# Two in-order queues reordered around a split-precision feed-forward layer, and a third pair of operand slots between its down passes

## What is computed

```
def swiglu(h, w_gate, w_up, w_down):
    return (jax.nn.silu(h @ w_gate) * (h @ w_up)) @ w_down
h = rms_norm(x, ffn1_norm[i])
x = x + 0.5 * swiglu(h, ffn1_w_gate[i], ffn1_w_up[i], ffn1_w_down[i])
```

## Time and profile before

| | us |
|---|---|
| timed runs, median (lowest to highest) | 914.07 (912.55 to 914.72) |
| profiled execution, its own time | 912.49 |
| its span, first to last instruction | 910.7 |
| DVE, ACT, POOL busy in it | 541.8, 496.5, 475.3 |

### The profile page before, as it was taken

The page is one execution under the profiler, slowest core; times in us unless marked ns, Lnnn a source line. Parts: engine busy times, 40 slices in busy tenths (PEclk is TensorE's granted clock), DMA queues, the critical chain, the costliest instruction groups (busy, mean ns, idle before and its releaser), DMA issues.

```text
span 910.7 us, 15441 instructions
## 1 busy us (share of the span) xinstructions
PE 893.5 (98%) x5462; PEld 798.7 (88%) x5462; DVE 541.8 (59%) x819; ACT 496.5 (55%) x777; POOL 475.3 (52%) x228
## 2 busy tenths in 40 slices
PE   9989999999999999999999999999999999989998
PEld 7779999999988778887788879999999988878887
DVE  7586766676422733778958586667666522652552
ACT  5765666566433633668834756556655533433451
POOL 0446666666554364266665346666665564355430
PEclk9999999999999999999999999999999999999999
DMA  7523333333333244221324233333333253223311
GB/s 200 160 59 115 115 92 98 110 115 92 109 122 92 70 115 102 60 81 48 70 70 120 65 93 93 101 106 114 92 106 103 90 162 93 91 92 93 94 69 46
DMA packets 131049, 89.33 MB, mean 98 GB/s; under 512 B 11552, under 2 KB 116296, under 8 KB 131016
## 3 DMA queue, kind: packets, MB, share of 16 engines
q1 hardware_dynamic: 131000, 88.90, 32.9%
q10 hardware_dynamic: 16, 0.00, 0.0%
HBM read 86.80 MB, written 2.10 MB: 98 GB/s over the span
## 4 chain that ended last, share of the span: by engine, by line
PE 86%; DVE 7%; ACT 4%; issue 2%; DMA 0%; SPq 0%; DVEq 0%; ACTq 0%
PE bank L1586 28%; PE bank L1587 28%; PE bank L1588 28%; PE bank L1601 1%; DVE wx_lo L1117 1%; ACT act_f L579 1%; DVE x_t L1194 1%; ACT w_hi L530 1%; DVE tmp L1192 1%; PE bank L1857 1%; DVE w_lo L1083 1%; DVE act_f L1129 0%; ACT tmp L575 0%; DMA raw<-in_ffn_w_up 0%; DVE h_lo L1022 0%
## 5 line engine op out<-in xcount | busy, mean ns | idle before, releaser
L405 POOL TENSOR_TENSOR w_lo<-raw,w_hi 128x1024 fp32r<-128x1024 f32 x85 | 219.2, 2587 | 246.1 <-ACT w_hi L530 246.1
L1586 PE MATMUL bank<-h_hi,w_hi 128*128 128x256 f32 (+1 forms) x700 | 228.2, 326 | 3.9 <-DVE w_lo L1083 3.9
L1588 PE MATMUL bank<-h_hi,w_lo 128*128 128x256 f32 (+1 forms) x700 | 226.8, 324 | 0.0
L1587 PE MATMUL bank<-h_lo,w_hi 128*128 128x256 f32 (+1 forms) x700 | 226.8, 324 | 0.0
L1117 DVE TENSOR_TENSOR wx_lo<-act_f,wx_hi 128x1024 fp32r<-128x1024 f32 x44 | 65.7, 1497 | 145.7 <-ACT wx_hi L631 145.6
L1586 PEld LDWEIGHTS bank<-h_hi,w_hi 128*128 128x128 f32 x700 | 133.2, 190 | 16.0 <-DVE w_lo L1083 4.8
L1588 PEld LDWEIGHTS bank<-h_hi,w_lo 128*128 128x128 f32 x700 | 133.3, 190 | 10.7
L1586 PE MATMUL bank<-wx_hi,w_hi 128*128 128x512 f32 x352 | 137.9, 392 | 4.9 <-DVE wx_lo L1117 4.9
L1587 PEld LDWEIGHTS bank<-h_lo,w_hi 128*128 128x128 f32 x700 | 133.3, 190 | 10.0
L1587 PE MATMUL bank<-wx_lo,w_hi 128*128 128x512 f32 x352 | 137.7, 391 | 0.0
L1588 PE MATMUL bank<-wx_hi,w_lo 128*128 128x512 f32 x352 | 137.5, 391 | 0.0
(11 more groups left out here) (232 smaller groups left out, 1891.0 us busy)
## 6 DMA issues: line engine op xcount, KB each, us to landing
raw<-in_ffn_w_down SPq DMA_DIRECT2D x44, 512.0 KB, 3.7
raw<-in_ffn_w_gate SPq DMA_DIRECT2D x42, 512.0 KB, 3.8
raw<-in_ffn_w_up SPq DMA_DIRECT2D x42, 512.0 KB, 3.8
raw<-in_w_ple_gate SPq DMA_DIRECT2D x8, 512.0 KB, 3.7
...
```

Of the source, the lines that this page charges most:

```text
L405: pool.tensor_tensor(w_lo[:, slot, :], raw[:, slot, :], f32(w_hi[:, slot, :]), ALU.subtract).then_inc(w_ready, 1)
L1586: nc.tensor.matmul(dst, a_hi, b_hi, start=first, stop=False, skip_group_check=more)
L1587: nc.tensor.matmul(dst, a_hi, b_lo, start=False, stop=False, skip_group_check=more)
L1588: return nc.tensor.matmul(dst, a_lo, b_hi, start=False, stop=last, skip_group_check=more)
```

## The change

- Seam, ACT: the eight h_gained run as one block, so that the splits of chunks 6 and 7 come behind all eight; the copies for the weight sums (rstd, stage, u, g, sa) come ahead of the x_rounds and silu(2), and u_round ahead of g_round.
- Seam, DVE: x3 and x2 come ahead of plain_up(1), then sums(2, 0) and u_rest; x4, the x_rests and block 2 of the plain part follow. plain_up(2) stands ahead of x_rest(2).
- Meet: a third pair of buffers, wx_hi[:, 2] and wx_lo[:, 2], which the seven-block pairs use for g and which is free by then, takes chunk 11. act_split(11) needs no wait; act_split(12) waits for chunk 9 and act_split(13) for chunk 10, each one chunk earlier than before; from 14 on the slots alternate again, and act_split(ch) waits for chunk ch - 2. On DVE act_rest(13) stands ahead of the four updates and act_rest(14) behind the four h_rests. On ACT act_split(14) stands ahead of split(15), counted in down chunks, and split(16) follows it. The loops of the second pass are written out.

The slots, and the waits of act_split:

```
+        def act_slot(ch):
+
+            return ch % 2 if ch < DH else 2 if ch == DH else (ch + 1) % 2
...
+                if ch < 2:
+                    act.wait_ge(w_used, c0 + GU - 2)
+                elif DH < ch < DH + 3:
+                    act.wait_ge(w_used, c0 + GU + ch - 2)
+                elif ch != DH:
+                    act.wait_ge(w_used, g + c0 + GU - 1)
```

ACT and then DVE at the seam:

```
-                for d in range(HALF):
+                for d in range(KD):
                     h_gained(n, d)
                 split(c0 + SLOTS + 2)
-                for d in range(HALF, KD):
-                    h_gained(n, d)
                 split(c0 + SLOTS + 3)
                 silu(n, 1, tmp[:, 1, :])
-                x_round(n, 0)
-                x_round(n, 1)
-                silu(n, 2, tmp[:, 0, :])
-                x_round(n, 2)
...
                 stage(n, c0, 2, 0)
+                act.wait_ge(w_used, c0 + SLOTS + 1)
+                u_round(n, c0, 2, 0)
                 g_round(n, c0, 2, 0)
                 sa_round(n, c0, 2, 0)
-                u_round(n, c0, 2, 0)
+                x_round(n, 0)
                 sb_round(n, c0, 2, 0)
+                x_round(n, 1)
+                silu(n, 2, tmp[:, 0, :])
+                x_round(n, 2)
```

```
-                plain_up(1)
...
+                plain_up(1)
+                sums(2, 0)
+                u_rest(2, 0)
...
                 x_rest(1)
+                plain_up(2)
                 x_rest(2)
-                plain_up(2)
-                sums(2, 0)
-                u_rest(2, 0)
```

ACT and then DVE at the meet:

```
-                step(DH - 2)
-                step(DH - 1)
-                act_split(n, c0, DH + 2, DH % 2)
+                act_split(n, c0, DH)
+                act_split(n, c0, DH + 1)
+                split(ahead + DH - 2)
+                act_split(n, c0, DH + 2)
+                split(ahead + DH - 1)
                 for d in range(HALF):
                     h_round(n * 2 + 1, d)
                     if n == 0:
                         h_square(1, d)
+                act_split(n, c0, DH + 3)
                 split(ahead + DH)
```

```
+                        act_rest(DH + 2)
...
-                        if half == 0 and i == 2:
-                            act_rest(DH + 2, DH % 2)
...
+                    if half == 0:
+                        act_rest(DH + 3)
```

More of the change, by code:

```diff
@@ L669, in pair @@
                     else:
-                        act_split(n, c0, 0, 0)
+                        act_split(n, c0, 0)
                     keep(n, q, p, 1)
@@ L678, in pair @@
                         split(c0 + GU)
-                        act_split(n, c0, 1, 1)
+                        act_split(n, c0, 1)
                     if staging:
@@ L697, in step @@
                     if s < 2 * DH - 2:
-                        act_split(n, c0, s + 2, s % 2, q)
+                        act_split(n, c0, s + 2, q)
                     split(ahead + s, slot, q)
@@ L711, in ffn_scalar @@
                         h_square(1, d)
+                act_split(n, c0, DH + 3)
                 split(ahead + DH)
-                if n == 0:
-                    for s in range(DH + 1, 2 * DH):
-                        step(s)
-                else:
-                    with act.Fori(0, (DH - 3) // SLOTS) as quad:
-                        for j in range(SLOTS):
-                            step(DH + 1 + j, quad, (ahead + DH + 1 + j) % SLOTS)
-                    for k in range(2):
-                        act.wait_ge(p_turned, k + 1)
-                        nc.scalar.activation(pt_hi[:, k, :], bank[k][:], ACT.Copy).then_inc(p_hi_done, 1)
-                    step(2 * DH - 2)
-                    step(2 * DH - 1)
+                split(ahead + DH + 1)
+                for s in range(DH + 2, 2 * DH):
+                    if n and s == 2 * DH - 2:
+                        for k in range(2):
+                            act.wait_ge(p_turned, k + 1)
+                            nc.scalar.activation(pt_hi[:, k, :], bank[k][:], ACT.Copy).then_inc(p_hi_done, 1)
+                    step(s)
                 for d in range(HALF, KD):
@@ L1150, in pair @@
                     else:
-                        act_rest(0, 0)
+                        act_rest(0)
                         dve.wait_ge(act_made, (n + 1) * NF - 1)
@@ L1159, in pair @@
                     if not following:
-                        act_rest(1, 1)
+                        act_rest(1)
                     fast_up(q, p)
@@ L1172, in ffn_vector @@
                     if half == 0:
-                        act_rest(2, 0)
-                    lead = 3 if half == 0 else DH + 3
-                    with dve.Fori(0, (DH - 3) // SLOTS) as quad:
-                        for j in range(SLOTS):
-                            act_rest(lead + j, (lead + j) % 2, quad)
-                    if half == 0:
-                        act_rest(DH, DH % 2)
-                        act_rest(DH + 1, (DH + 1) % 2)
-                    elif n == 1:
+                        act_rest(2)
+                        with dve.Fori(0, (DH - 3) // SLOTS) as quad:
+                            for j in range(SLOTS):
+                                act_rest(3 + j, quad)
+                        act_rest(DH)
+                        act_rest(DH + 1)
+                        act_rest(DH + 2)
+                    else:
+                        for ch in range(DH + 4, 2 * DH):
+                            act_rest(ch)
+                    if half and n == 1:
                         for k in range(2):
```

10 lines of the change are left out of this document (5 added, 5 removed).

## The result

| kernel | median of the timed runs, us | lowest to highest | profiled execution's own time | its span |
|---|---|---|---|---|
| before | 913.56 (4 runs) | 912.55 to 914.72 | 912.49 | 910.7 |
| changed | 908.63 (4 runs) | 908.23 to 909.02 | 908.90 | 907.1 |

The changed kernel takes 0.9946 of the time before (95% interval 0.9928 to 0.9963), 4.9 us less. The forecast was 5.2 us less, 908.9. It started from 914.07, which is the upper of the two middle runs of the four; their median is 913.56.

A forecast was written before the change was run, and what follows sets the result against it. The prediction took PE, busy 893.5 of 910.7 us, as the bound, leaving only its idle and low-clock time to gain. -2.5 - 4.5 + 0.9 + 0.9 = -5.2 us took 914.07 to 908.9, range 905.5 to 911.

The forecast's parts named there:

- The meets, -2.5 and -4.5: Meets of FFN1 and FFN2: act_rest(14) ends before PE wants it, both pauses close, saving 2.5 and 4.5 us.
- rival B: FFN1's meet closes only in part: POOL takes the port first, PE stands 1.5 us, 910.4 in all; chance 0.10.
- Rival D: Meets: act_rest(14), queued behind four h_rests that lose turns to POOL, makes PE wait again; slower, 916.0; chance 0.04.
- The seams, +0.9 each: Seams of FFN1 and FFN2: PE's restart comes 0.9 us later in each, from turns lost between DVE and POOL.
- turns of 2.2, 0.3, 2.3 and 2.2 lost: FFN1's seam: four waits, in us, as DVE operations with two SBUF tensors and POOL subtractions take turns at the port.
- Why the turns are lost: Seams: chunk 6's split comes 2.45 us later, and POOL's work falls among DVE's port operations; four turns against two.
- The end of the seam: Seams: the moment of PE's restart moves the cost one for one; 10.67 and 10.66 us follow it to the last wait.
- The clock at the seam, 0: Seams: the low clock costs nothing, as the chain of the other engines covers it; 0 us.
- Rival C: FFN2's seam: the longer pause lowers the clock and the time is not given back, +1.7 us, 910.6; chance 0.06.
- Rival A: Seams close as well because the four lost turns do not come about: 900 to 903 us; chance 0.10.
- The sum: Whole kernel: meets and seams together give -5.2 us, profiled execution 907.3, median 908.9.

The follow-up runs named there:

- e6_meet_swap: Kernel before, two slots kept, with only act_split of chunk 14 moved ahead of the splits of weight chunks 15 and 16: 905.89 us.
- e7_slot_only: Changed kernel with the old seam orders and the split of weight chunk 15 again ahead of act_split(14); third slot and DVE's meet order stay: 908.83 us.
- e3_g_late: Changed kernel with one ScalarE row moved: g_round stands behind silu(2), not ahead of sa_round: 902.26 us.
- e10_split_back: Changed kernel with ScalarE's first seam edit undone, a weight-chunk split again between the two halves of h_gained: 907.62 us.
- e8_fine_waits: Changed kernel with TensorE's single wait for three x rests ahead of the pair loop split into separate waits inside it: 907.66 us.
- e2_seam_only: Kernel before with only the new order of both engines at the seams, its meets as they were: 915.94 us.

## Why the prediction came out right, step by step

**The meets, -2.5 and -4.5.** Right in mechanism and size: -2.62 and -4.52, with the low clock behind FFN2's meet gone. act_rest(14) was to start at 315.4 and take 1.2; it started at 317.83 and took 1.22, later by the 0.73 and 1.73 that TensorE itself is late there; GpSimd asked 0.26 behind it, for the 0.2 of rival B, and came second. Rival D's turns at the h_rests did not come, for the reason given against it. What the forecast did not see is that one of the three edits does it. It gave each a part; e6_meet_swap shows that the order of two rows on ScalarE is enough for all but 0.4 us, and e7_slot_only that without it some 3 us come back.

**The seams, +0.9 each.** The sign and the mechanism were right, the size too small: +1.09 and +1.04, and in this trace 0.64 more in FFN1 for the clock. The working was good to 0.1 us. It has the third x_rest end at 58.8 and the trace, less its 0.73, at 58.78; it lists turns of 2.2, 0.3, 2.3 and 2.2 lost, and the rows show 2.2, 0.4, 2.2 and 2.2 (3.44, 1.05, 3.42 and 3.41 in place of 1.22 or 0.69). What failed is the step that compares: "The same steps on the old order give 57.97, where the trace has 57.75, so I take the difference, +0.9". The working was 0.2 late on the old order and not on the new one, so its error didn't cancel. With the trace's own end of u_rest, 57.70, it is 1.08.

**Why the turns are lost.** The forecast named two reasons, the split of chunk 6 coming 2.45 later, and GpSimd's work falling among DVE's. The second holds (e3_g_late), the first is refuted: e10_split_back puts the first split back and D doesn't move. The places of g_round on ScalarE and of u_rest on DVE decide.

**The end of the seam.** The forecast took the moment of TensorE's restart for it: "What a seam costs is moved one for one by the moment of the restart". The pause grew by 1.4 and 1.3, not 0.9 (forecast: to 4.0 and 2.0, measured 4.5 and 2.4), since there are 0.33 to 0.34 us between the end of the third x_rest and the first matmul behind a wait that stands ahead of the loop. If the step were right, the seams would cost 1.4 and 1.3. They cost 1.09 and 1.04, as DVE's plain_gate(3) doesn't wait for TensorE's restart; e8_fine_waits, which restarts 1.3 earlier and gains nothing, shows it. The equal 10.67 and 10.66 had come from a chain that started at the end of u_rest, which was also TensorE's releaser, and the two can't be told apart in the trace before.

**The clock at the seam, 0.** Right for a spell of 3.41 us, wrong for the one that came, 6.83 us, which cost 0.64. The likely reason is that a slowed TensorE eats first into its waits for DVE and ScalarE in the first pair, and only what is left over shows. By the distances of TensorE's matmuls in FFN2 of this kernel, where no spell lies, these waits come to some 1.9 us. The 1.7 us that a spell of 3.41 takes fit into that; of the 2.7 that 5.49 us at half clock take, an estimate leaves 0.8, near the measured 0.64. The Trainium skill, "TensorE: Matmul & The Clock Gate" (Terms), prices throttled time at its length times (1 - K/N), at half clock an estimate of 3.4 us for this spell. The trace agrees at the meet of FFN2 before and in e2_seam_only at that of FFN1 (1.7 and 1.6 us for 3.41), where TensorE is the bound, and not at the seam. Rival C did not come: FFN2's longer pause drew no spell in the trace of the changed kernel, and in that of e10_split_back it drew one of 3.4 us, at no cost.

**Rival A** did not come: the turns were lost as forecast. But its price for a kernel without most of them, 900 to 903, was right: moving one row of ScalarE gives it, e3_g_late at 902.3.

**The sum.** The median came out at 4.9 less against 5.2. That it is so near is in part luck. The profiled execution was forecast at 907.3 and took 908.90, 3.6 less and not 5.2. Of the 1.6 between, 0.7 lie at the start of the program, which the change doesn't touch, and 1.0 at the seams (0.3 for the turns, 0.64 for the clock); the meets give 0.1 back. The medians hide this, as the four runs before alone spread over 2.2 us.
